# A two-block float32 network on one Trainium2 core: the outputs of a state-space tile put ahead of the next tile's lag and state products

## The chip, the cores and the metric

One Trainium2 chip, one of its cores. The metric is device time in microseconds (us), the median over runs of the whole program. Engines are called by their names: TensorE (PE in the profile), VectorE (DVE), ScalarE (ACT), GpSimd (POOL); DMA transfers are issued by queues on SyncE (SP) and ScalarE.

## The reference

One token block of 256 x 2048 float32 goes through a first block (a state-space mixer, then an MLP) and a second block (convolution and spatial gating, FFN, Fourier mixing, FFN). Only the mixer is touched here. It is a linear recurrence over groups of 16 channels with 64 complex states each, forward and backward, over 256 context tokens and then 256 tokens of its own:

```python
def s5_scan(u, lam_bar, b_bar, s0, reverse):
    bu = jnp.einsum('btgh,gph->btgp', u, b_bar)
    first = -1 if reverse else 0
    bu = bu.at[:, first].add(lam_bar * s0)
    a = jnp.broadcast_to(lam_bar, bu.shape)
    _, states = lax.associative_scan(_lin_rec_combine, (a, bu), axis=1, reverse=reverse)
    return states
...
for direction in range(2):
    reverse = direction == 1
    ...
    st_ctx = s5_scan(uc_ctx, lam_bar, b_bar, s0, reverse)
    s_ctx_final = st_ctx[:, 0] if reverse else st_ctx[:, -1]
    st_lat = s5_scan(uc_lat, lam_bar, b_bar, s_ctx_final, reverse)
    y_lat = y_lat + jnp.einsum('btgp,ghp->btgh', st_lat, c_mat).real
...
z = jax.nn.gelu(y.reshape(h.shape).astype(h.dtype))
a, g = jnp.split(z @ w_glu, 2, axis=-1)
return a * jax.nn.sigmoid(g)
```

## The kernel before, in words

The program is written out by hand, one instruction list per engine, with semaphores between them. Every engine works its own list strictly in order. The state-space mixer takes the first part of the program, up to about 465 us of 3553; the rest is dense products (lines 439 and 440) that the change does not touch.

**Tiles and chunks.** The 2048 channels are 16 tiles of 128 (8 groups of 16). Time is cut into chunks of 8 tokens. Inside a chunk the recurrence is a fixed 8-lag filter (a Toeplitz matrix); between chunks a state is carried. For a tile n the steps are:

- GpSimd, `powers_of_c(n)`: the output matrix times the powers of the recurrence, into `cpow` (two buffers, n % 2), six operations recorded at line 1841; then `phases(n)`, seven operations into `pt`. `powers_of_c(n)` waits for `y_done` of tile n-2, because that tile's outputs read the same `cpow` buffer.
- VectorE, `powers_of_b(n)`: the input matrix times the powers, into `bpow`, eleven operations at line 1539. TensorE transposes them (`transpose_e`, line 1234), ScalarE copies them to `ew` (line 1413).
- TensorE, `lag_blocks(n)` (line 1247, 32 matmuls in the trace): needs `cpow` of tile n and `ew`'s copies, gives the 15 lag blocks in PSUM bank 5 (`k_done`).
- VectorE, `copy_lags(n)` (lines 1717 to 1719): lag blocks to `rw` (`r_sb`). SyncE then sends `rw` to DRAM (line 1108) and reads it back eight times into `tw` (line 1113), which spreads it into the Toeplitz matrix (`toeplitz(n)`, `t_in`).
- TensorE, `states(n)` (line 1263, 64 matmuls): what each chunk adds to the state, PSUM banks 1 and 2 (`v_done`). It waits for `s_done` of tile n-1, which frees these banks.
- VectorE, `rotate(n)`: the carry over chunks as two scans (lines 1787 and 1789) between rotations, into `st` (`s_done`).
- TensorE, `outputs(n)` (lines 1277 and 1280, 16 and 64 matmuls): Toeplitz product plus state product, bank 6 (`y_done`). It waits for `s_done` and `t_in` of tile n. ScalarE applies gelu; the result is transposed (line 1290) into `xin`, the operand of the next product.

**The round.** TensorE's list is a loop over k from -1 to 15. Round k holds the lag and state products of tile k+1, the outputs of tile k, then products with the modulation weights (`ada_rows`, line 1188, waiting for 1 MB loads of `in_w_mod`, issued by ScalarE), the preparation of tile k+2 (`spread_modulation` L1213, `select_c` L1179, `transpose_x` L1221, `transpose_e` L1234), and in rounds 0 to 3 one more set of modulation rows (`mod_rows`). VectorE's list for round k is `rotate(k)`, `copy_lags(k+1)`, a small `finish(k-1)`, `powers_of_b(k+2)`. So `copy_lags(k+1)` stands ahead of everything that VectorE does for tile k+1, and waits for `k_done`:

```python
            for k in range(KT):
                rotate(c0, k, k % 2)
                if k + 1 < KT:
                    copy_lags(c0, k + 1)
                if k:
                    finish(k - 1)
...
                if k + 2 < KT:
                    dve.wait_ge(s_done, k + 1)
                    powers_of_b(c0, k + 2)
```

Of the kernel before, what the change touches and what calls it, by code (L numbers as in the profile page):

```python
# [77 lines left out]
def two_layer_kernel(nc, a, out):  # L78
    ctx = ExitStack()
    with ctx:  # L80
# [155 lines left out]
        for v in par_src:  # L236
            n, done = v.shape[0], 0
            while done < n:
                k = min(n - done, P - at % P)
# [908 lines left out]
        def _(pe):  # L1148
# [24 lines left out]
            def select_c(n):  # L1173

                pe.wait_ge(c_tile, 32 * (n + 1))
                for ri in range(2):
                    for d in range(2):
                        for s in range(2):
                            ins = pe.matmul(ps[3][s * NST:(s + 1) * NST, (2 * ri + d) * 64:(2 * ri + d + 1) * 64],  # L1179
                                            craw[:, ri, d, :], sel_c[:, s * 64:(s + 1) * 64], start=True, stop=True)  # L1180
                ins.then_inc(c_sel, 1)

            def ada_rows(m, window, units=range(UK)):

                for kk in units:
                    pe.wait_ge(raw_ready[kk], 16 * (m + 1))
                    for q in range(UK):
                        ins = pe.matmul(ps[0][32 * q:32 * q + 32, :], cond[:, kk * UK + q, window:window + 32], raw[:, kk, q, :],  # L1188
                                        start=(m + kk == 0), stop=(kk == UK - 1), skip_group_check=True)
                    ins.then_inc(ada_unit, 1)  # L1190

            def mod_rows(b, v):
                ada_rows(MOD[b][v], 47 - (16 + 4 * b + 2 * v))

            def mod_columns(b):

                pe.wait_ge(ada_sb, b + 1)
                for r in range(NT):
                    ins = pe.matmul(ps[3][:, 256 + 4 * r:260 + 4 * r], adarow[:, r * P:(r + 1) * P], eye_c[:, 16 + 4 * b:20 + 4 * b],
                                    start=True, stop=True)  # L1200
                ins.then_inc(ada_col, 1)

            def ada_columns():

                pe.wait_ge(ada_sb, 5)
                for r in range(NT):
                    ins = pe.matmul(ps[3][:, KT * r:KT * (r + 1)], adarow[:, r * P:(r + 1) * P], eye_c[:, 0:KT], start=True, stop=True)
                ins.then_inc(ada_col, 1)

            def spread_modulation(n):  # L1210

                pe.wait_ge(mod_sb, n // 4 + 1)
                pe.matmul(ps[3][:, 288:320], spread, mrhs[:, n, :], start=True, stop=True).then_inc(mod_tr, 1)  # L1213

            def transpose_x(n):

                pe.wait_ge(xt_scaled, n + 1)
                if n > 1:
                    pe.wait_ge(y_gelu, n - 1)
                for g in range(GT):  # L1220
                    ins = pe.transpose(ps[6][:, g * 64:(g + 1) * 64], xt[:, g, :, :].rearrange("c j h -> c (j h)"), ident[0:64, 0:64])  # L1221
                ins.then_inc(u_tr, 1)

            def transpose_e(n, part):
                pe.wait_ge(bpow_done, n + 1)
                for q in (2 * part, 2 * part + 1):
                    if q == 0:
                        pe.wait_ge(mod_t, n + 1)
                        pe.wait_ge(c_sb, min(n + 2, KT))
                    if q >= 2:  # L1230
                        pe.wait_ge(e_sb, 4 * n + (q - 1))
                    for r in range(4):
                        ri, cb = divmod(4 * q + r, CB)
                        ins = pe.transpose(ps[3 + 2 * (q % 2)][:, r * P:(r + 1) * P], bpow[:, ri, cb, :], ident)  # L1234
                    ins.then_inc(e_tr, 1)

            def lag_blocks(n, b):

                pe.wait_ge(cpow_done, n + 1)
                pe.wait_ge(bd_sb, n + 1)  # L1240
                pe.wait_ge(lpp_sb, min(n + 2, KT))
                pe.wait_ge(e_sb, 4 * (n + 1))
                for d in range(2):
                    to = 7 * GRP * (1 - d)
                    for ri in range(2):
                        for kp in range(GT // 2):
                            ins = pe.matmul(ps[5][32 * kp:32 * kp + 32, to:to + P],  # L1247
                                            bd[:, 4 * d + kp, ri, :, :].rearrange("p s h -> p (s h)"), cpow[b][:, ri, 4 * d + kp, :],
                                            start=(d + ri == 0), stop=(d + ri == 2), skip_group_check=True)
                ins.then_inc(k_done, 1)  # L1250

            def states(n, b):

                pe.wait_ge(u_sb, n + 1)
                pe.wait_ge(e_sb, 4 * (n + 1))
                if n:
                    pe.wait_ge(s_done, n)
                for ri in range(2):
                    for cb in range(CB):
                        d, kp = divmod(cb, GT // 2)  # L1260
                        for s in range(2):
                            uv = u[b][:, 2 * kp + s, :].rearrange("p (q c) -> p q c", q=2)
                            ins = pe.matmul(ps[1 + ri][s * NST:(s + 1) * NST, cb * 64:(cb + 1) * 64],  # L1263
                                            ew[:, ri, cb, s * NST:(s + 1) * NST], uv[:, :, ::-1] if d else uv, start=True, stop=True)
                ins.then_inc(v_done, 1)

            def outputs(k, b):
                pe.wait_ge(s_done, k + 1)
                pe.wait_ge(t_in, 16 * L * (k + 1))
                for half in range(2):  # L1270
                    for term in range(5):
                        for q in range(4):
                            g = 4 * half + q
                            kp, s = divmod(g, 2)
                            o = ps[6][32 * q:32 * q + NCH, half * P:(half + 1) * P]
                            if term == 0:
                                ins = pe.matmul(o, u[b][:, g, NCH:2 * NCH], tw[:, g, :], start=True, stop=False)
                                continue
                            d, ri = divmod(term - 1, 2)
                            ins = pe.matmul(o, st[s * NST:(s + 1) * NST, ri, 4 * d + kp, :], cpow[b][s * NST:(s + 1) * NST, ri, 4 * d + kp, :],  # L1280
                                            start=False, stop=(term == 4))
                ins.then_inc(y_done, 1)

            def output_transposes(n):

                pe.wait_ge(y_gelu, n + 1)
                if n:
                    pe.wait_ge(z_lo, n)
                for i in range(L):
                    ins = pe.matmul(ps[7][:, 256 + i * NCH:256 + (i + 1) * NCH], zt[:, i, :], eye_c, start=True, stop=True)  # L1290
                ins.then_inc(z_tr, 1)
# [23 lines left out]
            mod_rows(1, 1)  # L1315

            for k in range(-1, KT):
                if k + 1 < KT:
                    lag_blocks(k + 1, (k + 1) % 2)
                    states(k + 1, (k + 1) % 2)  # L1320
                if k >= 0:
                    outputs(k, k % 2)
                if k + 1 < KT:
                    if k in (-1, 2, 4):
                        pe.wait_ge(ada_sb, {-1: 2, 2: 3, 4: 4}[k])
                    ada_rows(ADA[k + 1], 15 - (k + 1), (0, 1))
                if k in (-1, 2, 4):
                    mod_columns({-1: 1, 2: 2, 4: 3}[k])
                if k + 2 < KT:
                    spread_modulation(k + 2)  # L1330
                if k + 3 < KT:
                    select_c(k + 3)
                if k + 2 < KT:
                    transpose_x(k + 2)
                if k >= 0:
                    output_transposes(k)
                if k + 2 < KT:
                    transpose_e(k + 2, 0)
                if k + 1 < KT:
                    ada_rows(ADA[k + 1], 15 - (k + 1), (2, 3))  # L1340
                if k + 2 < KT:
                    transpose_e(k + 2, 1)
                if 0 <= k < 4:
                    mod_rows(2 + k // 2, k % 2)
                if k == KT - 2:
                    ada_columns()
# [594 lines left out]
```

## Time and profile before

| | us |
|---|---|
| median of 3 runs (lowest, highest) | 3557.34 (3548.33, 3568.26) |
| the profiled execution's own time | 3554.54 |
| its span, first to last instruction | 3552.7 |
| TensorE matmuls busy over the span | 3286.0 (92%) |
| VectorE busy | 2145.0 (60%) |
| ScalarE busy | 1380.7 (39%) |
| GpSimd busy | 480.5 (14%) |
| mean granted clock of TensorE | 0.955 of full |

The profiled execution is 2.8 us shorter than the median. Shares over the whole span say little about the mixer: it is an eighth of the span, and 321 of GpSimd's 480 us lie in the first 500.

### The profile page before, as it was taken

The numbers are of one execution on the slowest core, as the hardware profiler recorded it, in microseconds if no ns is written. First come the engines' busy times: TensorE is split into PE (matmuls) and PEld (weight loads), VectorE is DVE, ScalarE is ACT, GpSimd is POOL, SyncE is SP. The second block draws the span as 40 slices with busy tenths as digits, with TensorE's granted clock in tenths as the row PEclk, the third lists the DMA queues.
The fourth block names the chain that finished last, engine by engine and source line by source line (L and its number), as shares of the span: only waits on it lengthen the run. The fifth ranks groups of instructions, "written<-read, shape, count | busy, mean of one in ns | idle before, by whom it ended". The sixth has DMA issues, their size and how long they took to land.

```text
span 3552.7 us, 51801 instructions
## 1 busy us (share of the span) xinstructions
PE 3286.0 (92%) x21097; PEld 2763.3 (78%) x21097; DVE 2145.0 (60%) x1850; ACT 1380.7 (39%) x1385; POOL 480.5 (14%) x352
## 2 busy tenths in 40 slices
PE   5788899799999999886789999999999899999998
PEld 3445578688888888675678888888868788888887
DVE  7668755565555555699565555555644555555555
ACT  4446543433333333322234434433323344344332
POOL 2869900000000000096000000000000000000000
PEclk7888899899999999998799999999999999999999
DMA  9988875255555555344145555555524455555552
GB/s 299 305 282 257 260 243 175 91 184 189 185 189 182 190 186 189 107 142 148 36 154 178 186 190 182 186 189 189 177 92 142 142 186 184 187 187 189 189 183 89
DMA packets 351014, 643.22 MB, mean 181 GB/s; under 512 B 21599, under 2 KB 50359, under 8 KB 350519
## 3 DMA queue, kind: packets, MB, share of 16 engines
q1 hardware_dynamic: 309952, 561.68, 48.9%
q10 hardware_dynamic: 40951, 79.98, 6.6%
q8 instruction: 80, 1.31, 0.2%
q14 instruction: 31, 0.25, 0.0%
HBM read 637.54 MB, written 4.06 MB: 181 GB/s over the span
## 4 chain that ended last, share of the span: by engine, by line
PE 83%; DVE 6%; POOL 5%; issue 2%; DMA 2%; ACT 1%; SPq 1%; DVEq 1%; ACTq 0%; POOLq 0%
PE acc L439 49%; PE acc L440 25%; POOL cpow L1841 3%; DMA raw<-in_w_mod_dram 2%; POOL ptmp L1841 1%; PE acc L1263 1%; DVE z L943 1%; DVE w_lo L793 1%; PE acc L1280 1%; PE acc L521 1%; PE acc L533 1%; PE acc L464 1%; PE acc L1188 1%; PE acc L1247 1%; DVE hf L832 0%
## 5 line engine op out<-in xcount | busy, mean ns | idle before, releaser
L439 PE MATMUL acc<-xin,w_hi 128*128 128x512 f32 x5376 | 1915.2, 399 | 58.9 <-DVE xin L807 33.7
L793 DVE TENSOR_TENSOR w_lo<-raw,w_hi 128x2048 fp32r<-128x2048 f32 x484 | 1111.2, 2301 | 1079.0 <-ACT w_hi L640 1078.8
L440 PE MATMUL acc<-xin,w_lo 128*128 128x256 f32 x5376 | 1519.4, 283 | 0.0
L640 ACT ACTIVATE w_hi<-raw 128x2048 fp32r<-128x2048 f32 x484 | 926.8, 1917 | 1365.1 <-PE acc L440 1365.0
L439 PEld LDWEIGHTS acc<-xin,w_hi 128*128 128x128 f32 x5376 | 1017.2, 189 | 312.5 <-issue 35.6
L440 PEld LDWEIGHTS acc<-xin,w_lo 128*128 128x128 f32 x5376 | 1021.5, 190 | 0.0
L439 PE MATMUL acc<-hid,w_hi 128*128 128x512 f32 x2432 | 845.4, 392 | 0.0
L440 PE MATMUL acc<-hid,w_lo 128*128 128x256 f32 x2432 | 681.2, 280 | 0.0
L439 PEld LDWEIGHTS acc<-hid,w_hi 128*128 128x128 f32 x2432 | 455.1, 187 | 101.4
L440 PEld LDWEIGHTS acc<-hid,w_lo 128*128 128x128 f32 x2432 | 459.6, 189 | 0.0
L799 DVE TENSOR_REDUCE tmp<-acc 128x1024 f32<-128x2048 f32 x116 | 265.0, 2284 | 19.9 <-PE acc L440 19.9
L1188 PE MATMUL acc<-raw,cond 128*32 128x512 f32 x768 | 112.8, 700 | 45.5 <-DMA raw<-in_w_mod_dram 44.2
L674 ACT ACTIVATE hid<-tmp 128x1024 f32 x38 | 40.3, 1061 | 225.9 <-DVE tmp L863 131.1
L1064 POOL MEMSET y<- 128x4096 f32 x1 | 3.5, 3522 | 921.2 <-DVE xin L807 921.2
L1188 PEld LDWEIGHTS acc<-raw,cond 128*32 128x32 f32 x768 | 20.4, 119 | 106.0 <-DMA raw<-in_w_mod_dram 71.9
L1041 POOL MEMSET conv_in<- 128x120 f32 x1 | 0.2, 204 | 755.0 <-DVE xr L826 755.0
L943 DVE SCALAR_TENSOR_TENSOR z<-conv_in,par,z 128x256 f32<-128x256 f32 x180 | 101.1, 635 | 0.0
L1057 POOL TENSOR_SCALAR conv_tmp<-conv_in,par 128x256 f32<-128x256 f32 x60 | 88.5, 1475 | 0.0
L807 DVE TENSOR_TENSOR hid<-tmp,hid 128x1024 f32 x38 | 46.6, 1226 | 55.6 <-ACT hid L674 55.6
L1841 POOL TENSOR_TENSOR cpow<-cpow,ptmp 128x1024 f32<-128x1024 f32 x32 | 75.6, 2362 | 1.3
L1841 POOL TENSOR_TENSOR ptmp<-ct,lpc 128x1024 f32<-128x1024 f32 x32 | 62.0, 1936 | 70.6 <-PE acc L1280 47.1
L1442 ACT ACTIVATE u<-acc,modt 128x32 f32<-128x32 f32 x256 | 70.8, 417 | 0.7 <-PE acc L1221 0.2
(241 smaller groups left out, 2063.5 us busy)
## 6 DMA issues: line engine op xcount, KB each, us to landing
raw<-in_ffn_w_gate_dram SPq DMA_DIRECT2D x88, 1024.0 KB, 5.2
raw<-in_ffn_w_up_dram SPq DMA_DIRECT2D x88, 1024.0 KB, 5.1
raw<-in_ffn_w_down_dram SPq DMA_DIRECT2D x88, 1024.0 KB, 5.1
raw<-in_w_mod_dram ACTq DMA_DIRECT2D x76, 1024.0 KB, 9.7
raw<-in_w_mlp_in_dram SPq DMA_DIRECT2D x64, 1024.0 KB, 5.2
raw<-in_w_mlp_out_dram SPq DMA_DIRECT2D x64, 1024.0 KB, 5.1
raw<-in_s_w_glu_dram SPq DMA_DIRECT2D x32, 1024.0 KB, 5.3
raw<-in_ab_w_in_dram SPq DMA_DIRECT2D x32, 1024.0 KB, 5.3
```

Source lines behind the costliest of these rows:

```text
L439: pe.matmul(bank, w_hi[:, slot, w], operand[:, kt, :], start=(kt == 0), stop=False)
L440: ins = pe.matmul(bank[:, 0:TOK], w_lo[:, slot, w], operand[:, kt, 0:TOK], start=False, stop=(kt == UK * units - 1))
L640: act.activation(w_hi[:, slot, :], raw[:, slot, :, :].rearrange("p k n -> p (k n)"), ACT.Copy).then_inc(hi_ready, 1)
L674: act.activation(hid[:, ds(CH * chunk, CH) if not isinstance(chunk, int) else slice(CH * chunk, CH * (chunk + 1)), 0:TOK], tmp[:, half], A ...
L793: dve.tensor_tensor(w_lo[:, slot, :], raw[:, slot, :, :].rearrange("p k n -> p (k n)"), w_hi[:, slot, :].bitcast(F32), SUB).then_inc(lo_re ...
L799: dve.tensor_reduce(dst, acc[:, 4 * half:4 * half + 4, :].rearrange("p a (t b) -> p a b t", t=2), AX.X, ADD).then_inc(folded, 1)
L807: return dve.tensor_tensor(dst[:, k, TOK:2 * TOK], src, dst[:, k, 0:TOK].bitcast(F32), SUB).then_inc(done, 1)
L943: dve.scalar_tensor_tensor(z[:, k, :], x, c, z[:, k, :], MUL, ADD).then_inc(conv_dve, 1)
L1057: pool.tensor_scalar(conv_tmp[:, step % 2, :], x, c, None, ALU.mult).then_inc(conv_mul, 1)
L1188: ins = pe.matmul(ps[0][32 * q:32 * q + 32, :], cond[:, kk * UK + q, window:window + 32], raw[:, kk, q, :], start=(m + kk == 0), stop=(kk ...
L1442: ins = act.activation(u[b][:, g, q * NCH:(q + 1) * NCH], ps[6][:, g * 64 + q * NCH:g * 64 + (q + 1) * NCH], ACT.Identity, bias=modt[:, 16 ...
L1841: return pool.tensor_tensor(o, x, y, op)
```

## The change

In TensorE's loop the call of `outputs(k)` moves from behind `lag_blocks(k + 1)` and `states(k + 1)` to ahead of them. No instruction is added or removed and no other engine's list is changed.

```diff
             for k in range(-1, KT):
+                if k >= 0:
+                    outputs(k, k % 2)
                 if k + 1 < KT:
                     lag_blocks(k + 1, (k + 1) % 2)
                     states(k + 1, (k + 1) % 2)
-                if k >= 0:
-                    outputs(k, k % 2)
                 if k + 1 < KT:
```

TensorE's list in a later round, before. `cpow` times `bd` are the lag products, `u` times `ew` the state products, `tw` times `u` and `cpow` times `st` the outputs; in brackets the semaphores that a row waits for:

```order
L1234 MATMUL acc<-consts,bpow 128x128 x3
L1247 MATMUL acc<-cpow_63,bd 32x128 [waits lpp_sb,e_sb,bd_sb,cpow_done]
L1247 MATMUL acc<-cpow_63,bd 32x128 x15
L1263 MATMUL acc<-u_71,ew 64x64 [waits s_done,e_sb,u_sb]
L1263 MATMUL acc<-u_71,ew 64x64 x31
L1277 MATMUL acc<-tw,u_72 32x128 [waits t_in,s_done]
L1277 MATMUL acc<-tw,u_72 32x128 x3
L1280 MATMUL acc<-cpow_64,st 32x128 x16
L1277 MATMUL acc<-tw,u_72 32x128 x4
L1280 MATMUL acc<-cpow_64,st 32x128 x16
L1188 MATMUL acc<-raw,cond 32x512 [waits raw_ready0]
```

The same place of the changed kernel:

```order
L1234 MATMUL acc<-consts,bpow 128x128 x3
L1277 MATMUL acc<-tw,u_72 32x128 [waits t_in,s_done]
L1277 MATMUL acc<-tw,u_72 32x128 x3
L1280 MATMUL acc<-cpow_64,st 32x128 x16
L1277 MATMUL acc<-tw,u_72 32x128 x4
L1280 MATMUL acc<-cpow_64,st 32x128 x16
L1247 MATMUL acc<-cpow_63,bd 32x128 [waits lpp_sb,e_sb,bd_sb,cpow_done]
L1247 MATMUL acc<-cpow_63,bd 32x128 x15
L1263 MATMUL acc<-u_71,ew 64x64 [waits s_done,e_sb,u_sb]
L1263 MATMUL acc<-u_71,ew 64x64 x31
L1188 MATMUL acc<-raw,cond 32x512 [waits raw_ready0]
```

The four output rows moved past the lag rows and the state rows; the lag rows, which waited for no `s_done`, now stand behind a row that does.

VectorE's list at the same place, the same in both kernels (from the end of `rotate(k)` over `copy_lags(k+1)` and `finish` to the start of `powers_of_b(k+2)`):

```order
L1539 TENSOR_TENSOR st<-turned,acc 128x128 [waits dve_step]
L1539 TENSOR_TENSOR st<-turned,acc 128x4x32
L1717 COPY rw<-acc 128x112 [waits r_out,k_done]
L1718 COPY rw<-acc 128x112
L1719 SCALAR_TENSOR_TENSOR rw<-s5c,par,acc 128x16
L1539 TENSOR_TENSOR xin<-acc,xin 128x8x32 [waits z_hi]
L1539 TENSOR_TENSOR acc<-acc,bb 128x512 [waits e_tr,lpp_sb,s_done]
```

Nothing moved here; the row at line 1717 waits for `k_done`, which the lag products set.

## Rows read from the trace of the kernel before

**Rows 1.** Waits from 270 to 460 us: who waited for whom, total us, times, longest
```profile
DVE rw L1717 <- PE acc L1247: 32.8, 9, 4.3
PE acc L1247 <- POOL cpow L1841: 24.2, 9, 3.2
POOL ptmp L1841 <- PE acc L1280: 10.4, 8, 1.7
```

**Rows 2.** Chain that ended last, one round: start us, us, what
```profile
300.82 1.93 POOL ptmp L1841
...
310.95 2.35 POOL cpow L1841
313.35 1.08 PE acc L1247 x32
314.43 3.38 PE acc L1263 x64
317.81 0.50 PE acc L1277 x8
...
319.67 1.05 PE acc L1280 x32
320.88 1.93 POOL ptmp L1841
```

**Rows 3.** TensorE's timeline: start us, us, line, operation, [idle before, releaser]
```profile
257.17 0.65 PE L1277 MATMUL acc<-tw,u 128*32 128x128 f32 x8
257.76 1.93 PE L1280 MATMUL acc<-cpow,st 64*32 64x128 f32 x32
...
329.68 1.06 PE L1234 MATMUL acc<-consts,bpow 128*128 128x128 f32 x8 [0.90 <-ACT ew L1413]
333.39 1.94 PE L1247 MATMUL acc<-cpow,bd 128*32 128x128 f32 x32 [2.65 <-POOL cpow L1841]
...
338.76 0.43 PE L1277 MATMUL acc<-tw,u 128*32 128x128 f32 x8
...
341.48 1.92 PE L1188 MATMUL acc<-raw,cond 128*32 128x512 f32 x16
```

**Rows 4.** VectorE's timeline, same columns
```profile
314.49 0.28 DVE L1717 COPY rw<-acc 128x112 f32<-128x112 f32 x1 [3.27 <-PE acc L1247]
...
322.62 0.69 DVE L1539 TENSOR_TENSOR bpow<-bpow,acc 128x512 f32<-128x512 f32 x1
...
330.37 0.87 DVE L1539 TENSOR_TENSOR st<-turned,acc 128x128 f32<-128x128 f32 x4
```

**Rows 5.** Stretches of 1 us: length, busy PE PEld DVE ACT POOL, PEclk, DMA, GB/s
```profile
314.00:315.00 1.00, 1.00 (x32) 0.80 (x26) 0.51 (x3) 1.00 (x5) 1.00 (x2) 0.83 1.07 366
...
317.00:318.00 1.00, 1.00 (x24) 0.82 (x20) 1.00 (x2) 0.00 (x0) 1.00 (x2) 0.50 1.04 391
...
338.00:339.00 1.00, 1.00 (x26) 0.84 (x24) 0.97 (x3) 0.00 (x0) 1.00 (x2) 0.72 1.06 382
```

**Rows 6.** DMA issues: queue, count, KB each, median us from issue to landing
```profile
tw<-r_scratch SPq DMA_DIRECT2D x128, 64.0 KB, 2.6
...
r_scratch<-rw SPq DMA_DIRECT2D x16, 120.0 KB, 6.2
```

**Rows 7.** SyncE's queue: start us, us, line, transfer
```profile
336.02 0.44 SPq L1108 DMA_DIRECT2D r_scratch<-rw  x1
345.32 4.24 SPq L1113 DMA_DIRECT2D tw<-r_scratch  x8
...
448.88 10.12 SPq L355 DMA_DIRECT2D raw<-in_s_w_glu_dram  x5
```

**Rows 8.** TensorE's timeline: lag products of rounds 1, 4 and 14
```profile
139.56 1.93 PE L1247 MATMUL acc<-cpow,bd 128*32 128x128 f32 x32 [2.91 <-POOL cpow L1841]
...
230.28 1.93 PE L1247 MATMUL acc<-cpow,bd 128*32 128x128 f32 x32
...
436.73 1.21 PE L1247 MATMUL acc<-cpow,bd 128*32 128x128 f32 x32 [3.24 <-POOL cpow L1841]
```

## The prediction

> **What bounds the kernel now.** I read the waits of the mixer's later rounds first, because the page's shares mix the mixer with 3000 us of dense products that the change leaves alone. Three waits stand in a ring [rows 1]: GpSimd waits for the outputs (10.4 us in 8 rounds), TensorE's lag products wait for GpSimd's `cpow` (24.2 us in 9), and VectorE's `copy_lags` waits for the lag products (32.8 us in 9). The first two are the loop that sets the pace; the third is slack of VectorE. The chain of waits says the same in order of time [rows 2]: `powers_of_c` from 300.82 to 313.30 (12.5 us), lag products 313.35, state products 314.43, outputs from 317.81 to 320.72, and GpSimd's next `powers_of_c` at 320.88. The lag products of round 4 start at 230.28 and those of round 14 at 436.73 [rows 8]: ends at 232.21 and 437.94, so ten rounds in 205.7 us, **20.57 us a round**.
>
> What TensorE puts on that ring is 313.35 to 320.72, 7.4 us in this round and 8.1 in the next (333.39 to 341.48) [rows 3]. The two differ by the clock: the granted clock falls in 314 to 315 and is 0.50 in 317 to 318 [rows 5], and in the next round the half clock (1.2 GHz for 2.4) ends only in 338 to 339. It fell each time after a sparse stretch of TensorE: waits of 0.90 and 2.65 us with 1.06 us of transposes between them [rows 3].
>
> **What the change takes out of the ring.** The outputs of tile k need nothing of tile k+1. Ahead of the lag products, they free `cpow` some 5 us earlier, and GpSimd, whose own work is 12.5 us of `powers_of_c` and at most 7.6 us of `phases` (313.30 to 320.88) a round [rows 2], is no longer waited for: its result comes 12.7 us after the outputs, and the next lag products are, as now shown, over 20 us after them. So the ring through GpSimd (20.57) is gone, and with it the state products as a part of the pace.
>
> **What it puts in place.** The lag products waited for no `s_done`; now they stand behind the outputs, which do. And VectorE holds `copy_lags(k+1)` ahead of `powers_of_b(k+2)` and `rotate(k+1)`. So VectorE's slack becomes a wait on every round, and this ring closes: end of `rotate(k)`, outputs(k), lag products, `copy_lags`, finish, `powers_of_b`, `rotate(k+1)`. Its terms:
>
> - VectorE from the start of `copy_lags` to the end of `rotate`: 314.49 to 331.24, 16.75 us, without a gap [rows 4].
> - Outputs at full clock: 338.76 to the next row at 341.48, 2.72 us [rows 3]. At half clock one quarter pair takes 0.59 and 1.9 us [rows 3], so the whole about 4.9.
> - Lag products: 1.08 at full clock [rows 2], 1.94 at half [rows 3].
> - Two hand-overs between engines, 0.14 together: VectorE's copy starts 0.06 behind the lag products' end (314.43, 314.49), and I take 0.08 for the other.
>
> At full clock that is 16.75 + 2.72 + 1.08 + 0.14 = 20.7; at half clock throughout 16.75 + 4.9 + 1.94 + 0.14 = 23.7. The ring is longer than the old one at either end of the bounds, by 0.1 or by 3.2 us.
>
> **Where between them.** TensorE would now be idle about 4 us ahead of the outputs: after the lag products come 2.0 to 3.4 us of state products and the same 10 us of other work as now (320.72 to 330.74 [rows 2, 3]), with `transpose_e` held by `bpow` (ready 8.8 us behind the lag products [rows 4]) and the last transposes done some 12.7 us behind them, against the rotation's end at 16.8. That is a sparser stretch than the 3.6 us of waiting in 4.7 that now costs the clock every round [rows 3, 5]. If the clock falls as in round 313, 1.45 us into the work and for 3.2 us, outputs and lag products take 5.3 instead of 3.8 us, 1.5 lost; if as in the next round, half until 5.3 us after the start, 2.3 are lost. The old pace does not tell which phase the new one meets; a fall later in the work costs less than 1.5, as it then reaches into the state products, which no longer count. I take 1.5: **22.2 us a round**.
>
> Of TensorE's clock the Trainium skill says, in TensorE: Matmul & The Clock Gate, section HAM oscillation, that a kernel whose bursts are separated by long enough waits pays the return to half rate again at every burst. The trace agrees in that each of the rounds read here has a stretch at 0.50; taken to its end (every burst starts and stays slow) it is the second rival below.
>
> **The sum.**
> - Rounds 0 and 1 gain. In round 1 the lag products wait 2.91 us for GpSimd's long start [rows 8], and the outputs now fit into that wait: 2.7 us earlier.
> - Rounds 1 to 3 are bound by the loads for `mod_rows`; there all three groups precede the next work in either order, which is worth nothing. But `powers_of_b` ends later by the outputs' 2.7 to 4.9 us and holds `transpose_e`, which stands ahead of the rows that free the load buffers. I take 2.7 lost over these rounds (bounds 0 and 5), so that with the gain nothing is left.
> - Round 4: the lag products ended at 232.21, 1.93 after their start at half clock [rows 8]. With the outputs first they end 5.3 us after that start, 3.4 later.
> - Ten rounds, from the lag products of round 4 to those of round 14, at 22.2 instead of 20.57: +16.3.
> - The end: the first dense product waits for its weights, whose loads SyncE issues at 448.88 [rows 7], behind the last read of the Toeplitz tables. That is 10.9 us behind the last lag products (437.94) now. In the new order it is 0.6 of copies, 6.2 for the send [rows 6] and 4.2 for the eight issues [rows 7]: 11.0, the same distance. Nothing.
>
> 0 + 3.4 + 16.3 = 19.7 us. On the profiled execution, 3554.5 becomes 3574.2; on the median of the runs, 2.8 us above it, 3557.3 becomes **3577**, slower by 0.55%. A measurement of this kernel can tell about 0.5% (18 us) from no change.
>
> **Rivals.**
>
> *The clock holds (no change).* If TensorE meets the outputs and the lag products at 2.4 GHz in most rounds, the ring is 20.7: ten rounds give 1.3, round 4 gives 2.8, the early rounds 0 or a gain of 2.7: +2 to +4, about **3560**. It decides from a loss under 1.3 us a round: below that the whole stays under 18 us. For it: the outputs stand at the start of the burst, and the clock in round 313 fell only 1.4 us into it. Against it: the waiting ahead of the burst gets longer, not shorter. Chance 0.25, with the upper part of it reaching 3570.
>
> *Half clock throughout.* 23.7 a round: 10 x 3.1 = 31, round 4 4.6, early rounds up to 2: +37, **3594**. For it: the round at 333.39 was slow for 5.3 us from its start. Against it: the recovery in the round before came 3.2 us in. Chance 0.12.
>
> *The Toeplitz round trip is late.* The table of tile k+1 must now be there when `rotate(k+1)` ends, 16.8 us behind the lag products; before, its outputs came 24 us behind them (314.43 to 338.76 [rows 2, 3]). It takes 0.6, then 336.02 to 345.32, 9.3 us until the reads can be issued [rows 7], 4.2 for the issues and 2.6 to land [rows 6]: 16.7, just in time, where the read was under load of the weight rows; with the median 6.2 it is 13.6. In the new order the send goes out when the round's loads have landed, so I expect the lower one. Were it 2 us late in each round, +20 more, **3597**. Chance 0.08.
>
> *GpSimd's loop stays or the rounds get shorter (faster).* The pace could fall under 20.57 only if VectorE did not wait for the lag products, and it does by its list. What could still come is the 2.7 us of round 1 and as much in round 0: 3552 at best without the ring. Chance 0.05.
>
> **How the numbers follow.** The forecast case, 22.2 with its own bounds of 21.7 to 22.9, is 3571 to 3585 and has 0.5. Range: from the clock-holds case at 3560 to 3595, which takes in the half-clock case. Of the forecast's half a fifth lies under 3575, so slower than 0.5% has 0.4 + 0.12 + 0.08 - 0.04 for the profile's error = 0.56; faster by over 0.5% has 0.03; within 0.5% the rest, 0.41.
>
> **What would show it.** In the profile of the changed kernel, from 270 us on: the wait of `powers_of_c` for the outputs (L1280) stays or grows to some 2.5 us a round; lag products no longer wait for `cpow`; the wait of `copy_lags` for L1247 grows from 3.6 to 4 us or more in every round; the chain of waits goes through VectorE's L1539 where GpSimd's L1841 stood. The distance between two lag products is near 22.2, with outputs and lag products 5.3 us together. The first dense product (L439) starts near 485 instead of 465. Wrong would be: rounds of 20.7 with outputs of 2.7 us (the clock holds); outputs starting later than 0.1 us behind the end of `st` (the Toeplitz table); or GpSimd still last ahead of the lag products.

## The result, and the profile after

| | before | after |
|---|---|---|
| median of the runs, us (lowest, highest, runs) | 3555.73 (3548.33, 3568.26, 6) | 3588.12 (3586.61, 3592.83, 6) |
| the profiled execution's own time | 3554.54 | 3587.56 |
| its span | 3552.7 | 3585.8 |
| first lag product of round 4 starts at | 230.28 | 244.18 |
| first lag product of round 14 starts at | 436.73 | 469.54 |
| first dense product (L439) starts at | 465.07 | 493.75 |

The changed kernel takes 1.0090 times as long, 95% interval 1.0070 to 1.0109: **slower by 32 us**, where 20 were forecast. The forecast of 3577 was 11 us short; 3588 lies in the range. Ratios here and below are of fast executions alone; one of all the executions was slow, 11240.81 us in `e8_before_loads`.

The three moments at the foot of the table say where it is. By round 4 the changed kernel is 13.9 us behind; ten rounds later 32.8; at the first dense product 28.7. The last 4.4 us of the 33.1 between the two spans lie in the dense products, which are the same in both kernels; from the start of L439 to the end they took between 3083 and 3094 us in the profiles of this document, and the six times of before alone spread over 19.9 us. So I count with the 28.7. In the experiments the start of L439 is the measure of the mixer, and the distance from the first lag product of round 4 to that of round 14 ("ten rounds") that of the late rounds: 206.45 before, 225.36 after. Both measures are read from one profiled execution of each kernel, and this can be one from the edge of its times; where it is, the text says so.

The waits of the changed kernel from 270 to 460 us, which answer to [rows 1] (who waited for whom, total us, times, longest):

```profile
DVE rw L1717 <- PE acc L1247: 42.9, 8, 8.9
POOL ptmp L1841 <- PE acc L1280: 31.6, 9, 6.1
...
PE acc L1277 <- DMA tw<-r_scratch: 11.1, 3, 4.6
...
PE acc L1277 <- DVE st L1539: 8.5, 5, 2.5
```

The wait of the lag products for `cpow` is gone from the list, GpSimd's wait for the outputs has grown from 10.4 to 31.6 us, VectorE's for the lag products from 32.8 to 42.9. GpSimd's ring is open, as forecast. The third row was in no list of before: the outputs wait for the Toeplitz table.

A round without and one with that wait, TensorE's timeline, to be read beside [rows 3]:

```profile
302.68 1.97 PE L1234 MATMUL acc<-consts,bpow 128*128 128x128 f32 x8 [1.57 <-DVE bpow L1539]
304.58 3.64 PE L1188 MATMUL acc<-raw,cond 128*32 128x512 f32 x16
308.15 1.09 PE L1234 MATMUL acc<-consts,bpow 128*128 128x128 f32 x8
312.05 0.65 PE L1277 MATMUL acc<-tw,u 128*32 128x128 f32 x8 [2.81 <-DMA tw<-r_scratch]
312.63 1.93 PE L1280 MATMUL acc<-cpow,st 64*32 64x128 f32 x32
314.49 0.63 PE L1277 MATMUL acc<-tw,u 128*32 128x128 f32 x8
315.05 1.08 PE L1280 MATMUL acc<-cpow,st 64*32 64x128 f32 x32
316.06 1.08 PE L1247 MATMUL acc<-cpow,bd 128*32 128x128 f32 x32
...
334.01 0.43 PE L1277 MATMUL acc<-tw,u 128*32 128x128 f32 x8 [1.15 <-DVE st L1539]
334.36 1.08 PE L1280 MATMUL acc<-cpow,st 64*32 64x128 f32 x32
335.37 0.42 PE L1277 MATMUL acc<-tw,u 128*32 128x128 f32 x8
335.73 1.08 PE L1280 MATMUL acc<-cpow,st 64*32 64x128 f32 x32
336.74 1.08 PE L1247 MATMUL acc<-cpow,bd 128*32 128x128 f32 x32
...
357.11 0.66 PE L1277 MATMUL acc<-tw,u 128*32 128x128 f32 x8 [3.67 <-DMA tw<-r_scratch]
```

From 316.06 to 336.74 the round is 20.68 us: outputs at full clock, 2.73 us, right behind the end of `st`. The next is 25.3: the table comes late and the outputs then run at half clock for 4.9 us. The ten distances, in order, are 23.91, 24.57, 23.40, 20.68, 25.27, 22.31, 20.67, 23.18, 20.68, 20.69. Four rounds are the full-clock ring of the forecast to 0.02 us. What the other six have above it is 18.6 us, and that is nearly all that the late rounds lost: 13.1 in the four with a late table, 3.9 in the second (it holds the modulation columns, below), 1.6 in the sixth.

### The profile page after: what moved, and what is told of

Its sections match the earlier page's. It is cut to its first block, busy times and chain, and to the rows that moved or that the text cites. A ratio compares the mean times of both kernels' runs of the same rounds, so it can differ in the third digit from the quotient of the medians.

```text
span 3585.8 us, 51801 instructions
## 1 busy us (share of the span) xinstructions
PE 3306.3 (92%) x21097; PEld 2763.5 (77%) x21097; DVE 2148.8 (60%) x1850; ACT 1381.7 (39%) x1385; POOL 480.3 (13%) x352
## 4 chain that ended last, share of the span: by engine, by line
PE 81%; DVE 9%; DMA 5%; issue 3%; SPq 1%; ACT 1%; DVEq 1%; ACTq 0%
PE acc L439 49%; PE acc L440 25%; DMA raw<-in_w_mod_dram 2%; DVE bpow L1539 1%; DVE acc L1539 1%; DMA tw<-r_scratch 1%; PE acc L1280 1%; DVE z L943 1%; DVE w_lo L793 1%; DMA r_scratch<-rw 1%; PE acc L521 1%; PE acc L533 1%; PE acc L1188 1%; PE acc L464 1%; SPq L1113 0%
## 5 line engine op out<-in xcount | busy, mean ns | idle before, releaser
L439 PE MATMUL acc<-xin,w_hi 128*128 128x512 f32 x5376 | 1915.8, 400 | 58.7 <-DVE xin L807 33.7
L439 PEld LDWEIGHTS acc<-xin,w_hi 128*128 128x128 f32 x5376 | 1017.5, 189 | 312.4 <-issue 35.6
L439 PE MATMUL acc<-hid,w_hi 128*128 128x512 f32 x2432 | 847.1, 393 | 0.0
L439 PEld LDWEIGHTS acc<-hid,w_hi 128*128 128x128 f32 x2432 | 455.3, 187 | 102.9
L799 DVE TENSOR_REDUCE tmp<-acc 128x1024 f32<-128x2048 f32 x116 | 265.0, 2284 | 19.9 <-PE acc L440 19.9
L1188 PE MATMUL acc<-raw,cond 128*32 128x512 f32 x768 | 127.2, 778 | 45.6 <-DMA raw<-in_w_mod_dram 44.4
L1234 PEld LDWEIGHTS acc<-consts,bpow 128*128 128x128 f32 x256 | 37.6, 178 | 52.6 <-DVE bpow L1539 28.8
L1717 DVE COPY rw<-acc 128x112 f32<-128x112 f32 x16 | 4.4, 274 | 122.2 <-PE acc L1247 122.2
L1234 PE MATMUL acc<-consts,bpow 128*128 128x128 f32 x256 | 47.3, 344 | 31.4 <-DVE bpow L1539 27.1
```

What stands on the lines that cost most here:

```text
L439: pe.matmul(bank, w_hi[:, slot, w], operand[:, kt, :], start=(kt == 0), stop=False)
L799: dve.tensor_reduce(dst, acc[:, 4 * half:4 * half + 4, :].rearrange("p a (t b) -> p a b t", t=2), AX.X, ADD).then_inc(folded, 1)
```

## The experiments

**Which rounds.** The new order in rounds 0 to 3 only, and from round 4 on only:

```diff
-                if k >= 0:
+                if 0 <= k and k < 4:          # second run: k >= 4
                     outputs(k, k % 2)
                 if k + 1 < KT:
                     lag_blocks(k + 1, (k + 1) % 2)
                     states(k + 1, (k + 1) % 2)
+                if 0 <= k and not (k < 4):    # second run: not (k >= 4)
+                    outputs(k, k % 2)
```

> Outputs first in rounds 0 to 3 only, the old order from round 4 on. Theory: the load-bound rounds lose because the lag products come later, so powers_of_b ends later, holds transpose_e on TensorE and with it the rows that free the load buffers; the lag products of round 4 started 9.8 us later in the changed kernel (240.1 for 230.3, its outputs counted first), so this one has all of that and nothing more: first dense product near 475 instead of 465, time 9 to 10 us over before. Rival, the step as forecast (early rounds worth nothing): first dense product at 465, time as before.

> The old order in rounds 0 to 3, outputs first from round 4 on. Theory: ten rounds at 22.5 us instead of 20.57, 3 us for round 4, 3 to 4 us won back at the end: first dense product 465 + 19 = 484, time 18 to 22 us over before; with the run above it adds up to the whole change (29 us in the mixer). Rival: the late rounds cost only what the full clock asks, 20.7 a round, and the early ones the rest: first dense product 470.

Early only: L439 at 478.75, +13.7; the time is 1.0034 of before (1.0021 to 1.0047), a median of 3569.1 beside 3556.9. Ten rounds 208.6. Late only: L439 at 481.51, +16.4; 1.0061 (1.0043 to 1.0079); ten rounds 225.1. The two shifts sum to 30.1, for 28.7 of the whole change. The late-only profile is the fastest of four executions, 11.5 us under their median, so its 16.4 may be low; the two ratios, 1.0034 and 1.0061, add up to the 1.0090 of the change within their intervals. So the early rounds, which the forecast had at nothing, hold over a third and up to almost half of the loss, and more than the 10 us that I expected after the first look. In the second run four of the ten rounds wait for a late table again, by 2.5 to 4.7 us; the rival for the late rounds (only what the full-clock ring asks, L439 at 470) falls.

**What the early rounds lose.** VectorE's four small operations on the modulation columns, before and after, both in round 3. Before:

```profile
203.64 0.17 DVE L1731 SCALAR_TENSOR_TENSOR mcol<-msum,par 128x8 f32<-128x8 f32 x1
203.84 0.29 DVE L1539 TENSOR_TENSOR mrhs<-mcol,s5c 128x128 f32<-128x128 f32 x1
```

After, VectorE and then GpSimd at the same time:

```profile
212.29 1.86 DVE L1731 SCALAR_TENSOR_TENSOR mcol<-msum,par 128x8 f32<-128x8 f32 x1
214.19 1.98 DVE L1539 TENSOR_TENSOR mrhs<-mcol,s5c 128x128 f32<-128x128 f32 x1
```

```profile
212.06 3.95 POOL L1841 TENSOR_TENSOR cpow<-ct,lpc 128x1024 f32<-128x1024 f32 x2
215.98 2.40 POOL L1841 TENSOR_TENSOR cpow<-cpow,ptmp 128x1024 f32<-128x1024 f32 x1
```

Eight columns took 1.86 us and 128 took 1.98, about the 1.93 of one of GpSimd's operations, and the second ends at 216.2, just behind the end of GpSimd's second (216.0). Before, GpSimd was idle there. The outputs ahead of the lag products start `powers_of_c` just when VectorE, now behind the lag products, comes to these columns. The edit puts them into VectorE's wait:

```diff
             for k in range(KT):
                 rotate(c0, k, k % 2)
+                if k in (0, 3, 5):
+                    modulation(cm, {0: 1, 3: 2, 5: 3}[k])
                 if k + 1 < KT:
                     copy_lags(c0, k + 1)
                 if k:
                     finish(k - 1)
-                if k in (0, 3, 5):
-                    modulation(cm, {0: 1, 3: 2, 5: 3}[k])
```

> The changed kernel with VectorE's modulation columns (four small operations in rounds 0, 3 and 5) put ahead of copy_lags, in VectorE's wait, where GpSimd is idle too. Theory: they took 4.0 us instead of 0.6 in rounds 3 and 5 because each waited for an operation of GpSimd to end; on the ring of waits, so 3.4 us each in rounds 3 and 5 and about 2 in round 0 come back: 6 to 9 us under the changed kernel, the operations at 0.15 to 0.3 us. Rival: they are long for another reason (the order or their data), and stay at 2 us each wherever they stand: no gain.

3572.15 us, 1.0046 of before (1.0032 to 1.006) against 1.0090 for the change; L439 at 477.58, 16.2 earlier than with the change. The outputs of round 4 start at 232.53 instead of 240.08: 7.5 us of the early loss come back. Of these, 4.3 come between the outputs of round 3 and those of round 4, beside the 3.4 by which the two operations above had grown; 3.2 are there by round 3. In round 0 the two long operations took 2.1 us in the changed kernel and 2.3 in the kernel before, so there they had not grown; whether it is their new place that gave the 3.2 is not shown. The late rounds take 217.6 instead of 225.4, so that the whole gain, 16 us, is more than the 6 to 9 expected. They hold round 5's columns (the four made that round 3.9 us longer in the changed kernel), and the number of late tables fell from four to two in this execution, which is chance as far as this run can tell. In the new place the columns are not free of GpSimd either, and that shows the mechanism best:

```profile
192.03 1.20 DVE L1731 SCALAR_TENSOR_TENSOR mcol<-msum,par 128x8 f32<-128x8 f32 x1
193.26 0.29 DVE L1539 TENSOR_TENSOR mrhs<-mcol,s5c 128x128 f32<-128x128 f32 x1
```

```profile
190.69 2.51 POOL L1841 TENSOR_TENSOR pt<-pt,ptmp 128x512 f32<-128x512 f32 x2
```

The first is long up to 193.2, where GpSimd's last operation ends, and the next takes its own 0.29. They cost nothing here only because VectorE waits for the lag products anyway. The rival of my expectation, long wherever they stand, is out.

The Trainium skill has this in SBUF — State Buffer, section SBUF: two separate sides: VectorE and GpSimd share a pair of SBUF ports as an exclusive lock, held for a whole instruction, and a VectorE instruction with two SBUF inputs needs it against a GpSimd instruction that reads SBUF. The trace agrees: these have two SBUF inputs and wait; the copies at L1717, which read PSUM, kept 0.27 us (317.21, beside GpSimd at work).

**The table, first try.** ScalarE's first two weight loads of a round (1 MB each) moved behind its copies to `ew`, from round 4 on:

```diff
                     modulate_u(k + 2, k % 2)
-                    ada_units(act, ADA[k + 1] + 1, (0, 1))
+                    if k < 4:
+                        ada_units(act, ADA[k + 1] + 1, (0, 1))
...
                     copy_e(k + 2)
+                    if k >= 4:
+                        ada_units(act, ADA[k + 1] + 1, (0, 1))
                     ada_units(act, ADA[k + 1] + 1, (2, 3))
```

> The changed kernel with ScalarE issuing the first two weight loads of a round (1 MB each) behind copy_e instead of between the copies of u, from round 4 on; so the eight reads of the Toeplitz table are ahead of them in the DMA queues. Theory: in five of the late rounds the outputs waited for a table that landed 8 to 9 us after its last issue because these loads ran beside it; without it every late round is on VectorE's ring. Lag products of round 4 to round 14: 208 to 212 us instead of 225 (10 x 20.7 and 3.4 for the modulation columns), time 12 to 17 us under the changed kernel. Rival, as forecast (the clock costs 1.5 us in each round, the table is in time): 222 us, at most 3 us under it. Rival: the loads are then late for their own products and the rounds get longer.

No gain: 3588.74, 1.0086 (1.0069 to 1.0103), ten rounds 224.95. (The tables that were late in the changed kernel are four of the ten, not five.) Eight of the ten rounds then took 20.7 to 22.9 us, but one took 28.8. SyncE's queue in that round:

```profile
336.52 0.60 SPq L1108 DMA_DIRECT2D r_scratch<-rw  x1
346.08 4.06 SPq L1113 DMA_DIRECT2D tw<-r_scratch  x8
```

The send of `rw` came 4 to 7 us behind the issues of four loads and the reads could be issued only 9.6 us later; the outputs waited 9.18 us. Later loads did not free the table, they moved the collision from its way back to its way out. And round 5 took 26.8, its four columns now 6.2 us on VectorE. The control, the same loads in the kernel before:

> Control: the kernel before with the same two loads behind copy_e from round 4 on. Theory: there the outputs come 24 us behind the lag products and the table is never late, so the loads' place changes nothing: lag products of round 4 to 14 in 205 to 207 us, time as before within 5 us. Rival: the loads' later issue shortens or lengthens rounds by itself.

1.0007 of before (0.9996 to 1.0019), ten rounds 208.15 (205 to 207 expected): 1.7 more than before and the table never late. There the place of the loads makes no difference in time that can be told from none.

**The table, second try: no load beside it.** The loads of rounds 4 to 13 are cut to 32 of 512 columns; the modulation rows computed from them are left out in this way, all instructions stay:

```diff
-                queue.dma_start(raw[:, k, :, :], w_mod[:, k * UK:(k + 1) * UK, col:col + UN]).then_inc(raw_ready[k], 16)
+                queue.dma_start(raw[:, k, :, 0:w], w_mod[:, k * UK:(k + 1) * UK, col:col + w]).then_inc(raw_ready[k], 16)
```

> The changed kernel, its weight loads of rounds 4 to 13 cut to a sixteenth of their columns (64 KB instead of 1 MB), so that the DMA engines are nearly free while the Toeplitz table goes out and comes back. Theory (late tables, not the clock, made the late rounds longer than 20.7): no outputs wait for the table from round 5 on; lag products of round 4 to 14 in 210 to 213 us (10 x 20.7 and 3.4 to 6 for the modulation columns of round 5) instead of 225. Rival, as forecast (the clock falls ahead of the outputs and costs 1.5 a round): 222 us and more, the outputs at 4 to 5 us instead of 2.7.

> Control: the kernel before with the same cut loads. Theory: its late rounds are GpSimd's ring, the table and the loads are hidden, so 205 to 207 us from the lag products of round 4 to those of round 14, as with full loads; what the cut gives to the first weights of the dense products at the end is 0 to 3 us. Rival: the loads hold the rounds of before too; then they fall under 203 us.

> The changed kernel with the cut loads and with the modulation columns ahead of copy_lags. Both causes beside VectorE's ring are gone, so the late rounds should be the ring alone: 10 x 20.7 = 207 us (206.5 to 208.5) from the lag products of round 4 to round 14, and these start at 236 to 238 as in the run with the modulation columns moved. Rival: another wait, or the clock, keeps them over 210.

With the change, ten rounds in 214.3 instead of 225.4, and a time of 1.0056 of before (1.0041 to 1.0072): no output waits for the table from round 5 on; eight rounds are 20.67, round 5 is 26.8 (the columns), one 22.2 (outputs partly at half clock, with no late table ahead of them). The kernel before with the same cut: 205.1 (206.45 with full loads), so its rounds were not held by the loads, and 0.9983 (0.9974 to 0.9992) in time. With the columns moved as well, each of the ten rounds is 20.66 or 20.67, **206.67 in all**. Two lag products of it and what leads to the second:

```profile
300.70 1.08 PE L1247 MATMUL acc<-cpow,bd 128*32 128x128 f32 x32
...
318.65 0.43 PE L1277 MATMUL acc<-tw,u 128*32 128x128 f32 x8 [1.14 <-DVE st L1539]
319.00 1.08 PE L1280 MATMUL acc<-cpow,st 64*32 64x128 f32 x32
320.01 0.43 PE L1277 MATMUL acc<-tw,u 128*32 128x128 f32 x8
320.37 1.08 PE L1280 MATMUL acc<-cpow,st 64*32 64x128 f32 x32
321.38 1.08 PE L1247 MATMUL acc<-cpow,bd 128*32 128x128 f32 x32
```

That is the new ring alone, and it is level with the old one (206.67 for 206.45); beside the control with the same cut (205.1) it is 1.5 us longer. The ratio of this kernel is 1.0018 (1.0007 to 1.0028). Its lag products of round 4 start 11.2 us behind those of the control, which is what is left of the early loss and what round 4 itself costs (L439 at 468.98, and 459.68 in the control).

**The clock.** Both edits above, and 14 extra transposes (into a part of bank 7 that nobody reads) at the end of TensorE's list in rounds 4 to 13, to keep it busy ahead of the outputs:

```diff
                 if k + 2 < KT:
                     transpose_e(k + 2, 1)
+                if 4 <= k < KT - 2:
+                    for r in range(14):
+                        pe.matmul(ps[7][:, 0:P], ident, ident, start=True, stop=True)
```

> The changed kernel with both: the modulation columns ahead of copy_lags, the first two weight loads behind copy_e from round 4 on; and 14 extra transposes (about 3.7 us, into a free part of bank 7, nobody reads them) at the end of TensorE's list in rounds 4 to 13, so that its clock does not fall while it waits for rotate. Theory: VectorE's ring at full clock is 20.7 and TensorE was idle for 1.2 to 2.6 us ahead of the outputs, so the extra work delays the outputs by 1 to 2.5 us each round: 217 to 230 us from lag products 4 to 14, the granted clock at 1.00 in the outputs. Rival (the clock is what costs): at 1.00 throughout the rounds fall to 20.7 or below, 207 us.

3576.32, 1.0046 (1.0028 to 1.0064); the profiled execution is the slowest of four, 9.1 us over their median. Ten rounds 217.4, between 21.1 and 22.6 each, never 20.7, as expected of work that stands in the way. The outputs ran at the full clock in all ten. The run mixes three edits, and the two moves were not run without the fillers, so it says only that outputs at the full clock behind fillers do not make the rounds short; it does not size the loss by the clock.

**The order between.** Lag products, outputs, state products, which gives GpSimd its early start without holding `copy_lags`:

```diff
                 if k + 1 < KT:
                     lag_blocks(k + 1, (k + 1) % 2)
+                if k >= 0:
+                    outputs(k, k % 2)
+                if k + 1 < KT:
                     states(k + 1, (k + 1) % 2)
-                if k >= 0:
-                    outputs(k, k % 2)
```

> Lag products, outputs, state products in this order. Theory (what counts is that copy_lags does not wait for the outputs, and that GpSimd is freed early): the ring through GpSimd loses the state products, 12.5 + 1.1 to 1.9 + 2.7 to 4.9 + 0.2 = 16.5 to 19.5, below GpSimd's own 19.3 of work; pace 19.5 to 20.0 instead of 20.57: 5 to 10 us under before. Rival (any delay of the state products or of v_done costs, as much as a delay of the lag products): as the changed kernel, 20 us and more over before.

0.9996 of before (0.9987 to 1.0005), a median of 3554.65 in 11 runs beside 3556.88: not to be told from before, though L439 starts at 457.64, 7.4 earlier; the profiled execution is the fastest of the eleven, 6.8 us under their median. Ten rounds 203.7, 20.4 a round, where I expected 19.5 to 20.0. The rival (any delay of the state products costs) is out. What may hold it, in its own waits from 270 to 440 us:

```profile
POOL ptmp L1842 <- PE acc L1280: 12.9, 6, 3.7
...
PE acc L1277 <- DMA tw<-r_scratch: 9.5, 4, 4.0
```

GpSimd still waits for outputs, and four of the outputs waited for the table, by up to 4.05 us. With the columns moved too, and with columns and loads moved:

> Full work: lag products, outputs, state products in this order, and the modulation columns ahead of copy_lags; the loads where they were. Theory: the order alone was level with before because four of its late rounds waited for the table; the modulation columns cost it little, since copy_lags is early there: first dense product at 455 to 458, time 0 to 8 us under before, within what can be told apart. Rival: as with the outputs first, these columns hold VectorE while GpSimd runs, and moving them gives 7 us and more: first dense product under 452.

> Lag products, outputs, state products in this order, with the modulation columns ahead of copy_lags and the first two weight loads behind copy_e from round 4 on. Theory: with the table in time, the outputs early and VectorE's list not waiting for them, the pace of the late rounds is GpSimd's own work, 19.3 to 19.8 us instead of 20.57: lag products of round 4 to 14 in 193 to 198 us, first dense product near 455, 8 to 12 us under before. Rival (the order lag, outputs, states was held by ScalarE's and TensorE's chain of copies, not by the table): no better than that order alone, first dense product 458.

0.9999 (0.999 to 1.0008), L439 at 464.13, ten rounds 205.35 with four waits for the table, the longest 6.36 us; and 1.0003 (0.9994 to 1.0012), L439 at 463.60, ten rounds 204.2 with none. Both expected more. So late tables were not all that held this order: in the second none is late, the ten rounds are within 1.2 us of the other two, and a copy of ScalarE comes last ahead of the lag products, 8 times:

```profile
PE acc L1247 <- ACT acc L1404: 23.9, 8, 3.1
```

The chain of that kernel runs through ScalarE's copies of `u` (4.4 us a round), to `ew`, and its issues of four loads, which now all stand ahead of the copy that the lag products wait for. No version found here that does the full work beats the kernel before.

## Why the prediction came out as it did

- **GpSimd's ring opens, VectorE's closes.** Right, in the waits and in the chain of the changed kernel.
- **The ring at full clock is 20.7 us.** Right: 20.67 to 20.69 in four rounds of the changed kernel and in all ten of the run with cut loads and moved columns. VectorE's 16.75, the outputs' 2.73 and the lag products' 1.08 are all there.
- **"TensorE would now be idle about 4 us ahead of the outputs", 1.5 us of clock in each round.** This step failed. The waits ahead of the outputs are 1.1 to 2.6 us where the table is in time. The wait that I had put there sits earlier: `transpose_e` waits 1.57 us for `bpow`, the granted clock falls there, and the rows behind it take 3.64 us instead of 1.92. In stretches of 1 us (length, busy PE, PEld, DVE, ACT, POOL, PEclk, DMA share, GB/s):

```profile
301.00:302.00 1.00, 0.11 (x1) 0.00 (x0) 0.93 (x3) 1.00 (x5) 0.97 (x1) 0.66 0.87 174
304.00:305.00 1.00, 1.00 (x8) 0.45 (x10) 1.00 (x3) 0.93 (x3) 1.00 (x1) 0.50 1.10 320
...
290.00:291.00 1.00, 1.00 (x36) 0.80 (x40) 0.00 (x0) 1.00 (x4) 0.00 (x0) 1.00 0.73 203
292.00:293.00 1.00, 1.00 (x40) 0.80 (x36) 0.00 (x0) 1.00 (x4) 0.07 (x1) 1.00 1.04 399
```

  Half clock at 304, where nothing that sets the pace runs; full clock in the outputs of 290 to 293. One of the ten rounds (22.31) lost to the clock alone, 1.6 us. Behind the four late tables the outputs ran mostly at half clock too and took 4.0 to 4.9 us instead of 2.73, 6.3 us more in all. So the clock did cost 7.9 us of the 15, but in five rounds and not in ten, and in four of them behind a late table; with no table late one such round was left (22.2 us, with the loads cut). That the term came near to what the late rounds lost is luck.
- **The Toeplitz table is late: given 0.08.** This rival took the place of that term. Four of the ten late rounds waited for it and stand 2.5 to 4.6 us above 20.67, 13.1 in all: 6.8 by which the table landed behind the end of `st`, and the 6.3 of half clock behind the wait. The forecast had both ends, 13.6 us and 16.7 against 16.8, and chose the lower on the ground that the round's loads would have landed. That was so only in part: at most sends one of them was still open, where before it was mostly three, and the send is quicker (median 3.6 us instead of 6.2). But the reads meet the next loads. SyncE's reads and ScalarE's loads in the round of 23.40 us:

```profile
299.33 3.83 SPq L1113 DMA_DIRECT2D tw<-r_scratch  x8
...
300.45 0.38 ACTq L1078 DMA_DIRECT2D raw<-in_w_mod_dram  x1
300.87 0.52 ACTq L1078 DMA_DIRECT2D raw<-in_w_mod_dram  x1
```

  The last read was issued at 302.68 and landed at 311.9. In the four late rounds the send took 4.8 to 6.2 us, and the last read was issued 1.9 to 3.8 us behind the next load; in the other six the send took 1.8 to 3.1, and the last read was issued ahead of that load, once 0.8 us behind it. The run with cut loads shows that the loads are the cause: no table late from round 5 on, and 11 us less in the ten rounds, although the columns took 2.3 us more in it.
- **"Rounds 0 and 1 gain", and with rounds 2 and 3 come to nothing.** Failed. The outputs of round 4 start 9.8 us later. 7.5 of it come back when the modulation columns are moved, 4.3 of them where the collision with GpSimd had made them longer. They are in no term: I had counted them with VectorE's list and not asked what GpSimd, released earlier, would do to them. In round 0 the outputs, expected to fit into a wait, started at 109.91, 8.2 us of waiting for the table. How the remaining 2.3 us divide over rounds 0 to 3 was not taken apart.
- **Round 4, 3.4 us.** From the start of the outputs to that of the lag products 4.1 us passed; counted to the ends of the lag products, as the forecast did, it is 3.2. (For the same step the rival of the holding clock has 2.8, where its own terms give 2.72 + 1.08 - 1.93 = 1.9, and the half-clock rival 4.6, where they give 4.9. Neither changes the sum.)
- **"The end: nothing."** A gain of 4.1: from the last round's lag products to L439 24.2 us instead of 28.3. Of it 3.0 lie ahead of the first load of the dense weights: the send was reckoned at 6.2 us and took 2.3, the eight issues took 5.0 instead of 4.2. The other 1.1 lie behind it and were not looked into.

The sum, start to start: 13.9 to round 4 (9.8 and 4.1), ten rounds 18.9 (ring 0.2, tables 13.1, columns 3.9, clock 1.6), end -4.1: 28.7. Direction and range were right; of the 19.7 forecast, 15 stood on a clock loss in every round that was not there, and the two causes that were (the collision with GpSimd and the late table) had no place or 8%.

## What to carry to other kernels

When a change releases an engine earlier, list what will run beside it at its new time: its partner on the shared SBUF ports, and the transfers that meet. A transfer that has just enough time on paper should get its chance by the loads issued during it, out and back, not by those done before it. A change of order that takes a full engine's wait away and puts the same work into another engine's loop may leave the loop's length where it was (206.67 and 206.45 us here, 206.67 and 205.1 with the loads cut in both) and still lose by everything that had been hidden before.

## What the runs showed of the hardware

- A VectorE operation on 8 columns with two SBUF inputs took 0.15 to 0.17 us alone, and up to 1.9 us beside GpSimd's 1.93 us operations, ending 0.02 to 0.15 us behind the end of one of them. The four small operations of a round (three of 8 columns, one of 128) took VectorE 0.7 us in round 3 of the kernel before and 6.2 in round 5 of the run with later loads.
- 120 KB from SBUF to DRAM took 1.8 to 3.5 us until they had landed with the loads cut to 64 KB (the run with the columns moved, from 261 us on), 9.3 with three 1 MB loads open beside them (336.02 in the kernel before), and 9.6 behind the four loads shown above.
- TensorE's granted clock fell at a wait of 1.57 us after lighter work (0.66 in 301 to 302, 0.50 in 304 to 305 of the changed kernel), not only at the longer ones, and was back at 1.00 in the outputs that followed in five of the ten rounds; where it falls matters more than how often.
